# Rows of x loaded as feature quarters to four quadrants and turned by VectorE, in a two-layer hybrid encoder

## What is computed

```
h = rmsnorm(x, mix_norm)
aq ak av | sz sxbc sdt | mq mk mv mo mi mf = split(h @ w_in)          # w_in: 1024 x 2848
x = x + concat(window_attention, bidirectional_ssd, bidirectional_mlstm) @ w_out
x = x + expert_choice_swiglu_moe(rmsnorm(x, ffn_norm))                # 16 experts
```

## Time and profile before

| | us |
|---|---|
| three runs | 2317.18, 2318.82, 2319.92 |
| median | 2318.82 |
| profiled execution, its own time | 2318.55 |
| its span | 2317.1 |
| TensorE matmuls busy | 2273.0 (98%) |
| VectorE busy | 1239.2 (53%) |
| ScalarE busy | 622.8 (27%) |
| GpSimd busy | 542.8 (23%) |

### The profile page before, as it was taken

How to read it: one execution, slowest core, us unless ns; L and a number is a source line. 1 busy time by engine, 2 the same in 40 slices (tenths; PEclk the granted TensorE clock), 3 DMA queues, 4 the chain that set the end, 5 groups by cost and what they waited for, 6 DMA issues and landing times.

```text
span 2317.1 us, 33010 instructions
## 1 busy us (share of the span) xinstructions
PE 2273.0 (98%) x12766; PEld 1613.8 (70%) x12766; DVE 1239.2 (53%) x2399; ACT 622.8 (27%) x1445; POOL 542.8 (23%) x552
## 2 busy tenths in 40 slices
PE   8999999999999999999999999999999999999998
PEld 6556587874556778887775665878755567888776
DVE  3554466586647344555236434765865463455542
ACT  3221233464332111111132212335633421111111
POOL 1003454144211111111110034532432111111111
PEclk9999999999999999999999999999999999999999
DMA  4002132221127988878530111312212279888883
GB/s 155 21 25 68 55 122 74 74 91 56 74 73 254 348 302 292 299 264 284 148 120 21 37 55 59 119 60 82 83 55 82 82 274 343 300 290 274 284 295 83
DMA packets 149653, 352.16 MB, mean 152 GB/s; under 512 B 9941, under 2 KB 38105, under 8 KB 149498
## 3 DMA queue, kind: packets, MB, share of 16 engines
q1 hardware_dynamic: 134234, 308.11, 37.1%
q0 software_dynamic: 15264, 41.95, 7.4%
HBM read 307.75 MB, written 42.28 MB: 151 GB/s over the span
## 4 chain that ended last, share of the span: by engine, by line
PE 93%; DVE 4%; DMA 1%; ACT 1%; issue 1%; POOL 0%; SPq 0%; DVEq 0%; ACTq 0%; POOLq 0%
PE ps L1842 89%; PE ps L2127 1%; PE ps L2188 1%; DVE HT L1784 1%; PE ps L1861 1%; DVE TMP L1248 1%; DMA HT<-h_sample,idxs 0%; PE ps L1894 0%; DVE HT L1248 0%; PE ps L2139 0%; DVE TMP L1257 0%; ACT SCR L1051 0%; DMA MID<-w_in 0%; DVE SCR L1248 0%; POOL SCR L753 0%
## 5 line engine op out<-in xcount | busy, mean ns | idle before, releaser
L1842 PE MATMUL ps<-MID,HT 128*128 128x512 f32 (+3 forms) x2560 | 694.2, 491 | 4.8 <-DMA MID<-w_in 3.0
L1842 PEld LDWEIGHTS ps<-HT,MID 128*128 128x128 f32 x4096 | 557.2, 191 | 16.4 <-issue 15.4
L1842 PE MATMUL ps<-HT,MID 128*128 128x160 f32 (+1 forms) x4096 | 560.5, 299 | 1.0 <-DVE HT L1248 0.9
L1842 PEld LDWEIGHTS ps<-MID,HT 128*128 128x128 f32 (+1 forms) x2560 | 293.7, 157 | 248.3 <-issue 207.7
L1842 PE MATMUL ps<-RING,HT 128*128 128x256 f32 (+2 forms) x1760 | 395.8, 392 | 1.7 <-DVE RING L1252 1.3
L1842 PEld LDWEIGHTS ps<-RING,HT 128*128 128x128 f32 (+1 forms) x1760 | 310.7, 189 | 83.5 <-issue 40.7
L1842 PE MATMUL ps<-HT,RING 128*128 128x512 f32 (+1 forms) x960 | 350.0, 522 | 0.0
L1842 PEld LDWEIGHTS ps<-HT,RING 128*128 128x128 f32 x960 | 180.2, 190 | 157.8 <-issue 149.8
L1784 DVE STREAM_TRANSPOSE HT<-HT 32x256 f32<-32x256 f32 x576 | 251.0, 436 | 18.3
L1257 DVE SCALAR_TENSOR_TENSOR HT<-HT,ps 128x160 f32<-128x160 f32 (+1 forms) x128 | 40.9, 319 | 397.1 <-ACT HT L1210 395.1
L850 POOL DMA_INDIRECT y_prompt<-SCR,idxp x32 | 50.5, 1578 | 583.1 <-ACT SCR L1220 562.2
(11 more groups left out here) (268 smaller groups left out, 2177.2 us busy)
## 6 DMA issues: line engine op xcount, KB each, us to landing
MID<-w_gate SPq DMA_DIRECT2D x32, 2048.0 KB, 9.4
MID<-w_up SPq DMA_DIRECT2D x32, 2048.0 KB, 15.0
MID<-w_down SPq DMA_DIRECT2D x32, 2048.0 KB, 16.2
RING<-w_in SPq DMA_DIRECT2D x20, 1024.0 KB, 5.3
SCR<-cs_rows SPq DMA_DIRECT2D x20, 1024.0 KB, 5.2
MID<-w_out SPq DMA_DIRECT2D x8, 1024.0 KB, 6.4
y_sample<-RING SPq DMA_DIRECT2D x16, 512.0 KB, 2.6
h_sample<-HT SPq DMA_DIRECT2D x16, 512.0 KB, 2.6
```

Source lines behind the costliest of these rows:

```text
L1842: return pe.matmul(out, a, b, start=start, stop=stop)
```

## The change

x of a chunk no longer lies with one token per partition. It is loaded in six blocks of chunks (`BLOCKS`: 0 and 1; 2; 3; 4 and 5; 6 and 7; 8 and 9), each by four DMAs: quarter b of the features (256) goes to partitions 32b to 32b+31, and each partition holds four (in a chunk) rows of that quarter. A 32x32 block transpose of VectorE then leaves feature 8p+k of the chunk's 128 tokens on partition p, for all k in one instruction. So the weights are loaded by `(p k)` in place of `(k p)`. TensorE's 160 transposes of x are gone.

A token's sum of squares now lies in four pieces on four partitions. ScalarE squares each chunk in four pieces, TensorE adds the quadrants with a matmul by `SAME` (`sum_squares`), VectorE takes the mean (`mean_blocks`), GpSimd the power for a whole block, and VectorE scales the four pieces by root and norm weight and turns the chunk (`turn_blocks`). Chunks 0 and 1 are turned unscaled (`turn_raw`) and scaled later in `HT` (`scale_first`, now 2048 columns); their units are scaled when ScalarE empties them, with the roots of `keep_roots`. In layer 0 ZG is loaded from ScalarE's own queue instead of SyncE's.

The diff, cut to its core:

```diff
+XW = D // 4
+BLOCKS = [(0, 2), (2, 1), (3, 1), (4, 2), (6, 2), (8, 2)]
...
+        XRAW = [VO[:, 3112 + D * c:3112 + D * (c + 1)] for c in range(2)]
...
-        ss, rs = tiny(NC), tiny(NC)
+        rs = tiny(NP)
+        SSB, RSB = tiny(4 * NC), tiny(4 * NC)
...
@@ SyncE
+        ZG_PARTS = ((0, 512, 256), (256, 2832, 16), (272, 1792, 16))
-                                             .rearrange("(k p) n -> p k n", p=P)).then_inc(zg_loaded, 16)
+                                             .rearrange("(p k) n -> p k n", p=P)).then_inc(zg_loaded, 16)
...
-                    def x_load(c, layer=layer):
-                        sp.dma_start(XN[c], layer_x(c, layer)).then_inc(x_loaded[c if c < 4 else 2 + c // 2], 16)
+                    def x_blocks(i, layer=layer):
+                        c, n = BLOCKS[i]
+                        prompt, sample = (xp, xs_in) if layer == 0 else (yp, ys)
+                        rows = prompt[c * P:(c + n) * P] if c < NP else sample[(c - NP) * P:(c - NP + n) * P]
+                        for b in range(4):
+                            sp.dma_start(MID[32 * b:32 * b + 32, pv_at + c * D:pv_at + (c + n) * D].rearrange("p (a w) -> p a w", w=XW),
+                                         rows[:, XW * b:XW * (b + 1)].rearrange("(a j) w -> j a w", j=32)).then_inc(x_loaded[i], 16)
...
-                        x_load(0)
                         sp.dma_start(cstt[:, :], cst[:, :]).then_inc(cst_loaded, 16)
                         load_parameters(0)
-                        load_zg(0)
-                        for c in range(1, NP):
-                            x_load(c)
+                        x_blocks(0)
                     else:
                         sp.wait_ge(scattered_s, seen["halves"])
-                    for c in range(NP, NC):
-                        x_load(c)
+                    for i in range(1, len(BLOCKS)):
+                        x_blocks(i)
...
-                        for c in range(NP):
-                            x_load(c, layer + 1)
+                        x_blocks(0, layer + 1)
@@ GpSimd
-                    for c in range(NC):
-                        pool.wait_ge(squared, c + 1)
-                        rroot(rs[:, c:c + 1], ss[:, c:c + 1], 1, 1.0 / D, EPS, rooted)
+                    for i, (c, n) in enumerate(BLOCKS):
+                        pool.wait_ge(mean_made, i + 1)
+                        r = RSB[:, 4 * c:4 * (c + n)]
+                        link(pool.tensor_tensor(r, r, halfn[:, 0:4 * n], ALU.pow), rooted)
@@ ScalarE
+                    if layer == 0:
+                        with nc.allow_non_contiguous_dma(reason="gate columns"):
+                            for at, c0, w in ZG_PARTS:
+                                act.dma_start(ZG[:, :, at:at + w], wi[0:D, c0:c0 + w].rearrange("(p k) n -> p k n", p=P)).then_inc(zg_loaded, 16)
+                    def square_blocks(c):
+                        if c == BLOCKS[BLOCK_OF[c]][0]:
+                            act.wait_ge(x_loaded[BLOCK_OF[c]], 64 * (layer + 1))
+                        for a in range(4):
+                            link(act.activation(XSF[:, KD * ZGW + XW * a:KD * ZGW + XW * (a + 1)], XN[c][:, XW * a:XW * (a + 1)], ACT.Square,
+                                                accum_out=SSB[:, 4 * c + a:4 * c + a + 1]), squared if a == 3 else act_chain)
...
-                    square(0)
-                    square(1)
-                    for c in range(2, NC):
-                        square(c)
-                        if c % 2 == 0:
-                            scale_x(c)
-                        if c >= 3:
-                            evac(c - 3)
+                    for c in range(NC):
+                        square_blocks(c)
+                        if c == 3:
+                            keep_roots()
+                        if c >= 4:
+                            evac(c - 4)
@@ VectorE
+                    def mean_blocks(i):
+                        c, n = BLOCKS[i]
+                        dve.wait_ge(ss_summed, i + 1)
+                        ts(RSB[:, 4 * c:4 * (c + n)], ps[:, 3 + i % 5, 0:4 * n], 1.0 / D, EPS, ALU.mult, ALU.add, to=mean_made)
+                    def turn_rows(c, rows):
+                        link(dve.transpose(hT[:, :, c * P:(c + 1) * P].rearrange("p k (a j) -> p a k j", j=32),
+                                           rows.rearrange("p (a i k) -> p a k i", a=4, k=KD)), ht_copied)
+                    def turn_raw(c):
+                        if c == 0:
+                            dve.wait_ge(x_loaded[0], 64 * (layer + 1))
+                        tt(XRAW[c].rearrange("p (a w) -> p a w", a=4), XN[c].rearrange("p (a w) -> p a w", a=4),
+                           GMIX.unsqueeze(1).to_broadcast([P, 4, XW]), ALU.mult)
+                        turn_rows(c, XRAW[c])
+                    def turn_blocks(c):
+                        for a in range(4):
+                            v = XN[c][:, XW * a:XW * (a + 1)]
+                            scaled = link(dve.scalar_tensor_tensor(out=v, in0=v, scalar=RSB[:, 4 * c + a:4 * c + a + 1], in1=GMIX,
+                                                                   op0=ALU.mult, op1=ALU.mult), wait=False)
+                        dve.wait_ge(dve_chain, scaled)
+                        turn_rows(c, XN[c])
...
-                    keep_ht(0)
-                    for c in range(1, NC):
-                        if c % 2 == 1:
-                            scale_x(c)
-                        keep_ht(c)
-                        if c == 3:
-                            scale_first()
+                    link(dve.tensor_copy(SAME.rearrange("p (j e) -> p j e", j=4), FOLD.unsqueeze(1).to_broadcast([P, 4, 32])))
+                    dve.wait_ge(rs_spread, 1)
+                    link(dve.tensor_copy(GMIX, ps[:, 2, 0:XW]))
+                    for c in range(NP):
+                        turn_raw(c)
+                    mean_blocks(0)
+                    mean_blocks(1)
+                    for i, (c, n) in enumerate(BLOCKS):
+                        if i == 0:
+                            continue
+                        dve.wait_ge(rooted, i + 1)
+                        turn_blocks(c)
+                        if i + 1 < len(BLOCKS):
+                            mean_blocks(i + 1)
+                        if n == 2:
+                            turn_blocks(c + 1)
+                    scale_first()
@@ TensorE
+                    def sum_squares(i):
+                        c, n = BLOCKS[i]
+                        pe.wait_ge(squared, c + n)
+                        mm(ps[:, 3 + i % 5, 0:4 * n], SAME, SSB[:, 4 * c:4 * (c + n)]).then_inc(ss_summed, 1)
...
-                            pe.wait_ge(ht_copied, 2 * g + 2)
+                            pe.wait_ge(ht_copied, g + 1)
...
-                    turn_x(0)
+                    spread_norm()
                     unit(0)
-                    pe.wait_ge(rooted, 1)
-                    mm(ps[:, 2, 0:P], rs[:, 0:1].to_broadcast([P, P]), ident).then_inc(rs_spread, 1)
-                    turn_x(1)
-                    for c in range(2, NC):
-                        turn_x(c)
-                        unit(c - 1)
-                    unit(NC - 1)
+                    sum_squares(0)
+                    sum_squares(1)
+                    half = KD // 2
+                    for c in range(1, NC):
+                        unit(c, 0, half)
+                        if c in (1, 2, 4, 6):
+                            sum_squares((1, 2, 4, 6).index(c) + 2)
+                        if c == 2:
+                            spread_roots()
+                        unit(c, half, KD)
```

76 lines of the change are left out of this document (34 added, 42 removed).

## The result

The changed kernel takes 2338.36 us (median of 4 runs, 2336.46 to 2340.81), the kernel before 2318.53 (2317.18 to 2319.92) beside it: ratio 1.0086, 95% interval 1.0069 to 1.0104, 19.8 us more. I had forecast 2320.5 in a range that ended at 2326.

A forecast was written before the change was run, and what follows sets the result against it. It took TensorE as the bound, matmuls filling 98% of the span. Nearly all of 16 us saved went into seven waits and a later unit 0: 2318.55 + 2.2 - 0.4 = 2320.3, as median 2320.5 us, range 2313.5 to 2326.

The forecast's parts named there:

- +2.2 us: Layer 0's head: its ten units would end on TensorE at 62.4 us instead of 60.2.
- -0.4 us: Layer 1's head: its ten units would end on TensorE at 1211.8 us instead of 1212.2.
- the 8 us a layer: TensorE time the removed transposes would free at each layer's head, if everything else is ready in time; 16 in all.
- I take 1.25: Price in us of one VectorE transpose of a 128x1024 chunk; upper bound 1.74.
- the later of ZG and block 0 lands at 11.5 ... I take 13.5: Layer 0's start: loads landed at 11.5 us, unit 0 starting at 13.5 where it was 10.06.
- Block 0 is issued at 1154.26 and lands near 1160: Layer 1's first x load; unit 0 would then run from 1162.7 to 1169.1, its delay hidden behind chunk 2.
- wait 2 x 1.6: TensorE waits 1.6 us each for chunks 5 and 7, the next block's mean standing between two turns.
- Wait 2.3: TensorE's wait before unit 2 of layer 0, for roots and the turn of chunk 2; 2.3 us.
- wait 1.0: TensorE's wait before unit 4 of layer 0, the root of block 3 starting only after chunk 3; 1.0 us.
- change of these two ends as the change of the total: Shifts of unit 9's end in both layers equal the total's change, since TensorE runs on without a gap.
- x arrives at half the rate: Rival: x loads over 32 partitions move 200 GB/s, both layers' heads end 2.2 us later; 2325 us, chance 0.23.
- Dearer turn or late ZG: Rival: transpose at 1.74 adds 3 us, ZG behind x up to 2.5; 2323.5 to 2326 us, chance 0.10.

The follow-up runs named there:

- e2: The changed kernel with VectorE's transpose reading contiguous elements, so features land in another order than the weights'; 2329.99 us, ratio 1.0052.
- e6: The changed kernel with layer 0's ZG loads on SyncE's queue behind block 0 instead of ScalarE's queue; 2336.84 us, ratio 1.0079.
- e10: The changed kernel with block 0 split in two, sums of squares moved earlier, ZG on SyncE's queue behind chunks 0 and 1; 2323.09 us, ratio 1.0022.
- e5: The changed kernel with the sums of squares for blocks (6,7) and (8,9) moved ahead of units 4 and 6; 2326.1 us, ratio 1.0036.
- e4: The changed kernel with both the contiguous transpose read of e2 and the 128-partition loads of e1; 2324.67 us, ratio 1.0032.
- e13: e12 with ScalarE's evacuation of unit 0 moved ahead of the squares of chunk 4; 2320.01 us, ratio 1.0008.
- e1: The changed kernel with each of a block's four x loads spread over all 128 partitions, same bytes and runs; 2335.37 us, ratio 1.0071.
- e3: The kernel before the change, with each x load split into four loads of 32 partitions in 4 KB runs; 2319.39 us, ratio 1.0008.
- e12: e10 with the step moved from the transpose's read to the write of the scaling before it; 2321.37 us, ratio 1.0017.
- e7: The changed kernel with the two upper quarters of every x block on ScalarE's queue, behind ZG in layer 0; 2348.85 us, ratio 1.0130.
- e9: The changed kernel with transposes reading without a step and weights loaded in finer pieces to match; 2358.02 us, ratio 1.0179.

## Why the prediction was wrong

The main failure is in the terms of the sum, and all at once: "+2.2 us" for layer 0 was +12.1, and "-0.4 us" for layer 1 was +9.6. The steps that failed are the price of the turn, the landing of ZG and of block 0, and the clock behind the waits, which had no term. The direction of the reasoning held: the 8 us a layer do not come through, because mean, root, scaling and turn stop TensorE before units 2, 4, 5 and 7. The waits are where I had put them, in layer 0 before units 2, 4, 5 and 7 and in layer 1 before 2, 5 and 7, and one more in layer 1 before 4. The sizes were wrong, nearly all to the same side.

- **"I take 1.25" for the transpose: failed.** 2.03 us, outside both bounds (1.22 and 1.74). I had argued from elements, and the rows read and write without a step, while this transpose reads every eighth element. That was in the diff, `(a i k)`. e2 prices the term at 8.4 us of the 19.8, a fall of the clock in it.
- **"the later of ZG and block 0 lands at 11.5 ... I take 13.5" for unit 0: failed.** 17.04. I had kept 349 GB/s for both. Loads of 32 partitions fill the engines at 193 to 231 GB/s, and ZG's narrow runs had to share with them until 16.99. I had 16 as the end of the bound. With ZG queued behind block 0 (e6) the 13.5 comes true, at 13.63.
- **"Block 0 is issued at 1154.26 and lands near 1160": failed** by itself: 8.3 us after its issue, because it is waited for as 1 MB, in four loads of 256 KB, at the lower rate, where the kernel before waited for the first 512 KB. In layer 1 I had called the later unit 0 hidden behind chunk 2; unit 0 came 11.9 us after x's issue instead of 6.5, and the cover was gone. e10's split gives unit 0 at 1168.45, 9.5 us after the issue.
- **"wait 2 x 1.6": right in place, short in size.** 2.10 and 2.09 in layer 0, 2.10 and 2.10 in layer 1, by the transpose: with 1.245 they are 1.33. I had seen that the mean of the next block stands between two turns; moving it is worth 12.3 us (e5).
- **"Wait 2.3" before unit 2, "wait 1.0" before unit 4:** 2.73 and 0.69 in layer 0. Layer 1 waits 2.73 and 1.71 there, where I had 2.5 and nothing before unit 4; the 2.73 ends with VectorE's turn of chunk 2, not with evac(0), so there the size was right by luck. evac(0) ends that wait of layer 1 where the turns or the roots come earlier (e2 4.00, e4 2.99, e10 3.87).
- **The clock behind waits: not in the sum.** I had the slow unit 0, from the earlier trace rows, and no other. The matmuls from unit 5 of layer 0 and from unit 7 of layer 1 take 1.7 us more each so, and unit 2's first half in layer 0 takes 2.81 instead of 2.19: 4.0 us of the 22.3.
- **"change of these two ends as the change of the total": nearly.** +12.1 in layer 0 became +14.0 at x's issue in layer 1. 1.2 of it is a wait for the gather of h_sample, 2.1 us where it was 0.9, and e13 has it too; why the gather comes later was not tried and stays open.
- **Prices that held:** the power for 8 columns 1.77 (I had 1.7), for 4 columns 1.01; squares 0.42; the scalings, 1.67 for four (I had 1.8); the weights by `(p k)`, at nothing. For TensorE's small matmuls I had 0.1 and 0.4 without a row: a sum in the middle of unit 4 takes 0.14 from start to start, and the sum and spread_roots in unit 2 together 0.68 in layer 1, 1.28 in layer 0.

Of the rivals, *x arrives at half the rate* was right in its mechanism (209 to 231 GB/s) and wrong in what it decides: e1 gives it 3.0 us and e3 1.5, both within what I had worked out for it (4.5). *Dearer turn or late ZG* was right in both of its halves, at once: its upper end, 2326, held both, but with the turn at 1.74 and unit 0 at 16, where 2.03 and 17.04 were measured. The chances treated as alternatives what were terms that can come together. Yet the sum of all of them, 2320.5 + 4.4 + 3 + 2.5 = 2330.4, is still 8 us short: the rest is the turn beyond its bound, the clock, and block 0 of layer 1, and those no rival held.

## What to carry to other kernels

Price an operation by a row with the same access pattern, not only the same size: a step in the read cost a VectorE transpose 63% here, and a step in the write of the scaling ahead of it less. When an operation is replaced by a longer chain over four engines, ask of each link what it stands behind in its engine's order; moving two small matmuls half a unit forward was worth 12.3 us, the cheaper transpose 8.4 and the faster loads 3.0. And if several terms of a sum are each uncertain to the same side, the range must take their sum.

## What the runs showed of the hardware

- A VectorE transpose of 128x1024 in fp32 takes 1.245 us reading without a step, 2.029 reading every eighth element. A scaling of 128x256 that writes with a step of 32 elements takes 0.53 us from start to start (2.12 for four, e12), without 0.42 (1.67 for four).
- Loads that write 32 partitions each, on one queue, move 193 to 209 GB/s in runs of 1 KB (the change, 18 to 28 us) and 221 to 229 in runs of 4 KB (e3), with the engines full; over 128 partitions it is 348 (e1) and 400 (before). Two queues that write opposite halves at once, in runs of 1 KB, reach 346 (e7).
- Issuing is not free of the engines' state: a load of 128 partitions by 1 KB takes 0.54 us to issue while they keep up and 4.2 when they do not (e9).
- After a wait of about 2 us TensorE's granted clock fell to 0.50 (1.2 GHz) in one stretch and did not in another with the same wait: 34 matmuls took 9.91 and 8.22 us. It fell behind 6 of 20 waits of 2.1 us and behind none of 12 of 1.3 us; among waits of one length, what decides stays open.
